# Attention layers of a two-block model: one group of softmax matmuls for each pair of heads

## The reference, cut to what matters

```python
for l in range(DEPTH_2):
    h = rms_norm(x, pre_norm_g[l]) * (1.0 + scale[:, None, :]) + shift[:, None, :]
    proj = h @ w_in[l]                       # q, k, v, g_att, u, b_gate, c_gate, g_conv
    att = dilated_attention(q, k, v, rel_bias) * silu(g_att)
    cnv = b_gate * short_conv(c_gate * u, conv_w[l]) * silu(g_conv)
    mix = concatenate([att, cnv], axis=-1) @ w_out[l]
    x = x + gate[:, None, :] * rms_norm(mix, post_norm_g[l])
```

## Time and profile before

| | |
|---|---|
| median of 3 runs | 815.71 us (815.12 to 815.75) |
| profiled execution, its own time | 816.1 us |
| span of the profiled execution | 814.3 us |
| PE busy | 801.9 us, 98% of the span |
| DVE / ACT / POOL busy | 592.0 / 417.1 / 144.2 us |
| mean granted clock of PE | 0.995 |
| loop of layer 0, of layer 1 (start of `scores(0)` to start of the last product) | 577.66 to 647.68 us, 714.63 to 785.84 us |

### The profile page before, as it was taken

The page is one execution under the profiler, slowest core; times in us unless marked ns, Lnnn a source line. Parts: engine busy times, 40 slices in busy tenths (PEclk is TensorE's granted clock), DMA queues, the critical chain, the costliest instruction groups (busy, mean ns, idle before and its releaser), DMA issues.

```text
span 814.3 us, 15551 instructions
## 1 busy us (share of the span) xinstructions
PE 801.9 (98%) x6350; PEld 775.7 (95%) x6350; DVE 592.0 (73%) x958; ACT 417.1 (51%) x710; POOL 144.2 (18%) x156
## 2 busy tenths in 40 slices
PE   9999999999999999999999999999999999999997
PEld 9999999999899999999999999999899999999986
DVE  6777766798687875788777779976667567567753
ACT  7544444445267565555444455436555454555541
POOL 3800000032220000020000004230245302035510
PEclk9999999999999999999999999999999999999999
DMA  9876776686336643458867779535544651744531
GB/s 335 302 257 220 237 251 237 217 298 191 104 118 207 197 122 101 155 178 291 282 230 261 253 231 341 184 105 207 153 158 129 183 161 47 258 156 131 155 104 52
DMA packets 45191, 158.84 MB, mean 195 GB/s; under 512 B 5040, under 2 KB 6576, under 8 KB 45120
## 3 DMA queue, kind: packets, MB, share of 16 engines
q1 hardware_dynamic: 45120, 157.85, 58.5%
HBM read 156.76 MB, written 1.06 MB: 194 GB/s over the span
## 4 chain that ended last, share of the span: by engine, by line
PE 80%; DVE 11%; ACT 5%; issue 3%; POOL 1%; DVEq 0%; POOLq 0%; ACTq 0%
PE ps L110 72%; PE ps L112 8%; DVE w L112 3%; ACT w L112 2%; DVE u L112 2%; DVE tmp L112 1%; DVE yg L112 1%; DVE cv L112 1%; ACT SW L112 1%; ACT L112 1%; ACT ytm L112 1%; POOL rst L112 1%; DVE Vs L112 0%; DVE g L112 0%; POOL hT L112 0%
## 5 line engine op out<-in xcount | busy, mean ns | idle before, releaser
L110 PE MATMUL ps<-u,w 128*128 128x256 f32 (+1 forms) x3887 | 502.1, 285 | 2.8 <-ACT u L112 0.8
L110 PEld LDWEIGHTS ps<-u,w 128*128 128x128 f32 x3887 | 483.0, 189 | 12.2 <-issue 2.8
L112 DVE TENSOR_TENSOR w<-raw,w 128x1024 fp32r<-128x1024 f32 x245 | 297.5, 1226 | 141.9 <-ACT w L112 141.5
L112 ACT CAST w<-raw 128x1024 fp32r<-128x1024 f32 x245 | 254.0, 1048 | 127.3 <-PE ps L112 121.8
L110 PE MATMUL ps<-h,w 128*128 128x272 f32 (+1 forms) x1000 | 130.0, 285 | 0.0
L110 PEld LDWEIGHTS ps<-h,w 128*128 128x128 f32 x1000 | 125.7, 188 | 0.1
L112 POOL TENSOR_TENSOR sqa<-sqa,sq 128x272 f32<-128x272 f32 (+1 forms) x16 | 20.7, 1294 | 322.4 <-ACT sq L112 322.0
L112 POOL TENSOR_SCALAR Sb<-Sb,st 128x256 f32<-128x256 f32 x32 | 45.0, 1424 | 89.1 <-DVE st L112 89.1
L112 DVE SCALAR_TENSOR_TENSOR acc<-adr,cact,acc 128x1024 f32<-128x1024 f32 x42 | 57.7, 1398 | 0.0
L112 ACT ACTIVATE si<-tmp 128x272 f32<-128x272 f32 (+1 forms) x44 | 18.7, 424 | 70.0 <-DVE tmp L112 70.0
L112 PE MATMUL ps<-u,w 128*128 128x256 f32 (+1 forms) x169 | 48.1, 285 | 0.0
(11 more groups left out here) (185 smaller groups left out, 746.8 us busy)
## 6 DMA issues: line engine op xcount, KB each, us to landing
raw<-wst SPq DMA_DIRECT2D x245, 512.0 KB, 4.6
adr<-wada SPq DMA_DIRECT2D x48, 512.0 KB, 4.1
Bt<-bias_rows SPq DMA_DIRECT2D x8, 192.0 KB
hT<-xT SPq DMA_DIRECT2D x4, 272.0 KB, 5.4
outT<-yg SPq DMA_DIRECT2D x4, 256.0 KB, 2.1
cs<-cst SPq DMA_DIRECT2D x1, 140.0 KB, 5.3
cs<-cst SPq DMA_DIRECT2D x1, 128.0 KB, 7.2
vc<-vec SPq DMA_DIRECT2D x1, 101.0 KB, 3.6
```

The lines of the kernel that those rows point to most:

```text
L110: fn()
L112: fn().then_inc(m[0], m[1])
```

## The change

`values(k)` leaves step 4k+7 (part 3) for step 4k+8 (part 0). `transposes` of the odd head leaves part 1 for part 0, directly behind that of the even head, and writes a bank that `take` gives from the rotation instead of bank 5, so that the two don't wait for each other's copy. In part 0 of pair k there now stand, one behind the other, the values of pair k-2, the eight transposes of pair k-1, and the scores of pair k. The number of instructions that compute stays as it was.

```diff
             def transposes(h):
-                i = h % 4
-                pe.wait(free[5], nrm[h])
+                i, bt = h % 4, (take() if h % 2 else 5)
+                pe.wait(free[bt], nrm[h])
                 for j in range(2):
                     for t in range(2):
                         mt = pe(partial(nc.tensor.transpose, 
-                            ps[:, 5, S * j + 128 * t:S * j + 128 * t + 128], Sb[:, i, t, 128 * j:128 * j + 128],
+                            ps[:, bt, S * j + 128 * t:S * j + 128 * t + 128], Sb[:, i, t, 128 * j:128 * j + 128],
                             ident))
                 sbr[i] = mt
-                ptm[h] = free[5] = act(partial(nc.scalar.copy, PT[:, h % 2, :, :],
-                                                          ps[:, 5, :].rearrange("p (j q) -> p j q", q=S)),
+                ptm[h] = free[bt] = act(partial(nc.scalar.copy, PT[:, h % 2, :, :],
+                                                          ps[:, bt, :].rearrange("p (j q) -> p j q", q=S)),
                                    mt, ptr[h % 2])
...
             for at_ in range(21):
                 k, part = at_ // 4, at_ % 4
-                if part in (0, 1) and 0 < k < 5:
-                    transposes(2 * k - 2 + part)
+                if part == 0 and k > 1:
+                    values(k - 2)
+                if part == 0 and 0 < k < 5:
+                    transposes(2 * k - 2)
+                    transposes(2 * k - 1)
                 if part == 0 and k < 4:
                     scores(k)
                 if part == 1 and k < 4:
                     weights2(k)
-                if part == 3 and 0 < k:
-                    values(k - 1)
```

## The result

The changed kernel takes 820.78 us (median of 6 runs, 819.85 to 820.97), against 815.60 us for the kernel before on the same chip. The ratio is 1.0063 with a 95% interval of 1.0052 to 1.0073: slower by 5.2 us. The forecast gave slower the greatest chance, and slower it is, but the size was wrong: 817.4, with a range that ended at 819.2.

The account below looks back on a forecast made before the run. PE, busy for 98% of the span, was taken to bound the kernel. Waits in pair 1 (+2.88 us) less the last values of layer 1 (-1.19) gave +1.69 on 815.71, so 817.4 us, range 816.1 to 819.2.

Parts of the forecast that it names:

- What the grouping saves on PE: nothing: Grouped matmuls in the loops: same matmuls and half-array borders as before, so 0 us saved.
- Rivals 3 and 4: Grouping saves at each of 14 returns to a block: 0.09 us (816.1, chance 0.14) or from 0.24 us (chance 0.05).
- A wait in pair 1 of each layer: Odd head's transposes in pair 1 wait for POOL's fourth multiplication: 1.44 us per layer, +2.88 in all.
- the 0.09 added for a first weight load: Part of the 1.44 us wait in pair 1: a first weight load that could not run ahead.
- The last values of layer 1: End of layer 1's loop: the last values fit in a gap of 1.18 us and leave the path, -1.19 us.
- Pairs 2 to 4: POOL's multiplications end before the odd transposes need them, with 1.1 us to spare, then 0.51; taken as 0.
- Rival 2: POOL also late in pairs 3 and 4, beside DVE subtractions, four places: 819.0, or 821.2 with a full subtraction; chance 0.14.

Follow-up runs that it names:

- grouped_act: Changed kernel with the four multiplications of a pair on ACT in place of POOL; 815.39 us against 814.97 before, ratio 1.0005.
- all_three: Changed kernel with the edits of pair1_apart, pool_first and cast_behind together; 813.88 us against 814.81 before, ratio 0.9990.
- Last_values_only: Kernel before with only the last values (pair 3) moved behind the last block; 814.04 us against 814.81 before, ratio 0.9992.
- pair1_apart: Changed kernel, but in pair 1 alone the odd head's transposes stay in part 1; 817.78 us against 815.16 before, ratio 1.0033.
- cast_behind: Changed kernel with the attention tile's cast and subtraction one step later, behind the weight cast on ACT; 816.52 us against 814.81 before, ratio 1.0020.
- pool_first: Changed kernel with DVE's weight subtraction behind the reciprocals waiting for POOL's first multiplication of the pair; 817.28 us against 815.16 before, ratio 1.0025.

## Why the prediction was wrong

**Right.** PE sets the end, and the loops account for 4.99 of the 5.2 us. *What the grouping saves on PE: nothing*: 0.04 us for a pair in grouped_act, and nothing in all_three. Rivals 3 and 4 fall with it. The Trainium skill (TensorEngine Tiling (Array Packing), Key Properties) ties a drain of the engine to a change of the tiling mode; the runs agree, since the values cost 0.17 us at their two borders, transposes nothing, and the changes of mode stayed four for each pair. *A wait in pair 1 of each layer*: 1.35 and 1.33 us for 1.44; PE starts 0.15 us behind POOL's end, and the 0.09 added for a first weight load doesn't show. *The last values of layer 1*: 1.19 us, as worked out. Last_values_only shows the last of these terms alone, and pair1_apart the wait of pair 1, together with the 0.15 of pair 2.

**The step that failed** is *Pairs 2 to 4*, where the text says "I take 0 for these four, with little air". They cost 0.15 (pair 2), 0.84 and 0.86 us in layer 0 and as much in layer 1, 3.7 us in all. With the 5.47 us of the earlier trace rows POOL was to end 0.51 us ahead of PE in pair 3; with the starts of the changed kernel it would have been 0.40 (614.92 + 5.47 = 620.39 on POOL; on PE 620.29 and the 0.50 that the first four transposes take behind values in cast_behind). But 5.47 was no property of the instruction: it was the outcome of an order between DVE and POOL, which the change moved at both ends. The four took 6.54. Late by 1.07 - 0.40 = 0.67, plus 0.15 of wake-up, is 0.82 us, where pairs 3 and 4 show 0.84 and 0.86. So the chain of the forecast held, with one wrong duration in it.

**Rival 2** was the result: its price for a full turn, 0.95 us in four places, or 821.2, lies 0.4 us off. That closeness is partly luck: it charged one whole subtraction of 1.22 us, and the 1.07 came as 0.43 and 0.64 from two places. It had 0.14, and the argument against it, that "in the order of before POOL already holds the turn", is what the change undid. I had looked at one end of POOL's time, where `at` leaves; that gave 0.64 us, once both moves were made. At the other end I had costed the ACT copy of the odd transposes only as a copy that frees a bank. It was also what kept DVE's subtraction 0.30 us behind POOL, and its leaving gave 0.43 us. It was there to be seen in the order of ACT, in the rows behind those that I showed: `PT<-ps` stood ahead of the very cast that this subtraction waits for. The rule of the Trainium skill (SBUF — State Buffer, Who interferes with whom) says that the first to start keeps the other out for its whole instruction. The runs agree only in part. In cast_behind and pool_first a multiplication that starts first by 0.13 us or more, with nothing of DVE's beside its start, lasts 0.92 or 0.93. But the second one of pool_first starts first by 0.05 and lasts 1.99, and the one of 2.21 in the earlier trace rows starts 0.28 ahead of the subtraction and still loses 1.3 us; another DVE instruction (`cw<-cu,vc,cw`) had started 0.12 us ahead of it. Nor does DVE lose a whole instruction: behind a multiplication of 0.92 us its subtraction takes 1.43 in place of 1.22.

What stays open: in pair 2 of each layer the four multiplications are as long as in pairs 3 and 4 (6.54 us), but cost 0.15 us, because no casts `m<-cw` and `m<-at` stand ahead of them; this was read from the rows and not tried by itself. A disturbed multiplication lasts 1.4 to 2.2 us. The traces show a rule for its end: in all 211 such multiplications of the eleven traces that have them on POOL, the end lies 0.71 to 0.81 us behind the end of a DVE weight subtraction. In pair 2 of the changed kernel that is 614.80 + 1.20 = 616.00 and 614.92 + 1.88 = 616.80. Which of the two gets the turn when their starts lie within 0.1 us stays open: 21 multiplications that started 0.05 or 0.06 ahead of a subtraction lost, three won.

## What to carry to other kernels

A duration on an engine that shares something with another is a fact of an order; when a change moves work on either engine, lay out the new order of starts and price it from rows in that order, not from the row at the same place. The slowest row of its kind is the least to allow for; here even that (6.13 us in pair 0, which gave 819.0) would have been too low. Check the slack at both ends of such a stretch, and for every copy or cast that leaves a place on a third engine ask what it was holding back. And before grouping matmuls, measure what a border costs: here transposes between blocks cost 0.11 us each and no border, so there was nothing to win, and the one gain of size (1.1 us) was work put into a gap where PE waited anyway.

## What the runs showed of the hardware that I had not expected

- The first POOL multiplication (128x256) of a pair lasts 0.92 or 0.93 us if DVE's subtraction of two SBUF inputs starts 0.13 to 0.30 us behind it, and 1.88 us if that starts 0.12 us ahead. The subtraction itself is stretched less: 1.43 and 1.25 us when it starts 0.13 and 0.30 behind, 1.20 when it starts ahead.
- A stretched multiplication ends 0.71 to 0.81 us behind the end of a DVE subtraction, whichever of the two started first.
- Adding a wait on DVE (pool_first) made the program 3 us faster than the changed kernel.
- Transposes, values and scores of one group follow each other without a loss beyond that of the half arrays: values to scores is 2.04 us with eight transposes between.
- The row of a wait can name the wrong releaser: "ACT PT" stood at waits that vanished when the multiplications left POOL. The end of the POOL row, 0.15 us ahead of PE's start (621.46 and 621.61), was the better witness.
